# Row sums of squares as two fp32r products between the pair of tiles and the third tile

## The reference

```python
def rms_norm(x, g):
    xf = x.astype(jnp.float32)
    y = xf * lax.rsqrt(jnp.mean(xf * xf, axis=-1, keepdims=True) + EPS)
    return (y * g.astype(jnp.float32)).astype(x.dtype)

def sqrelu_mlp(h, w1, w2):
    return jnp.square(jax.nn.relu(h @ w1)) @ w2

def swiglu_ffn(x, w_in, w_out):
    gate, up = jnp.split(x @ w_in, 2, axis=-1)
    return (jax.nn.silu(gate) * up) @ w_out
# x = x + mixer(norm(x)); x = x + mlp(norm(x)); ... h = h + 0.5 * swiglu_ffn(rmsnorm(h, g), w_in, w_out)
```

## Time and profile before

| what | us |
|---|---|
| median of three runs | 1545.5 (1544.36 to 1545.63) |
| the profiled execution | 1544.45 |
| its span, from first to last instruction | 1542.7 |
| PE busy | 1530.5 |
| DVE busy | 1045.6 |
| ACT busy | 849.7 |
| DMA, busy share of 16 engines | about 56% |

### The profile page before, as it was taken

How to read it: one execution, slowest core, us unless ns; L and a number is a source line. 1 busy time by engine, 2 the same in 40 slices (tenths; PEclk the granted TensorE clock), 3 DMA queues, 4 the chain that set the end, 5 groups by cost and what they waited for, 6 DMA issues and landing times.

```text
span 1542.7 us, 34843 instructions
## 1 busy us (share of the span) xinstructions
PE 1530.5 (99%) x12794; PEld 1492.5 (97%) x12794; DVE 1045.6 (68%) x1766; ACT 849.7 (55%) x1302; POOL 122.5 (8%) x123
## 2 busy tenths in 40 slices
PE   9999999999999999999999999999999999999999
PEld 8899999988999999999999999999999998999999
DVE  7777765644876557666787766668576657787764
ACT  6776654546655445555445555556555547665543
POOL 1830000045000000000000000000000033200000
DMA  7156666554666665656665655656555972065564
GB/s 257 59 135 195 193 190 203 167 174 138 194 195 197 193 192 191 193 194 200 190 207 193 200 191 191 206 186 206 194 192 192 235 206 66 16 204 193 193 199 151
DMA packets 80783, 280.51 MB, mean 182 GB/s; under 512 B 8880, under 2 KB 12464, under 8 KB 80688
## 3 DMA queue, kind: packets, MB, share of 16 engines
q1 hardware_dynamic: 76512, 273.77, 55.8%
q10 hardware_dynamic: 4176, 5.38, 1.8%
HBM read 277.53 MB, written 1.57 MB: 181 GB/s over the span
## 4 chain that ended last, share of the span: by engine, by line
PE 94%; DVE 4%; ACT 1%; issue 1%; DMA 0%; SPq 0%; ACTq 0%; DVEq 0%
PE psum L1800 27%; PE psum L1804 27%; PE psum L1801 27%; PE psum L1948 2%; PE psum L1950 2%; PE psum L1949 2%; PE psum L2190 1%; PE psum L2239 1%; DVE w_lo L1067 1%; PE psum L2135 0%; DVE scratch L1664 0%; PE psum L2013 0%; PE psum L2223 0%; PE psum L2003 0%; DMA raw<-tiles 0%
## 5 line engine op out<-in xcount | busy, mean ns | idle before, releaser
L579 ACT ACTIVATE w_hi<-raw 128x1024 fp32r<-128x1024 f32 x515 | 544.1, 1059 | 474.8 <-PE psum L1804 437.2
L1067 DVE TENSOR_TENSOR w_lo<-raw,w_hi 128x1024 fp32r<-128x1024 f32 x480 | 587.2, 1224 | 251.8 <-ACT w_hi L579 251.5
L1800 PE MATMUL psum<-xs,w_hi 128*128 128x256 f32 x1904 | 528.8, 278 | 1.0 <-DVE w_lo L1729 0.8
L1801 PE MATMUL psum<-xs,w_hi 128*128 128x256 f32 x1904 | 526.0, 276 | 0.0
L1804 PE MATMUL psum<-xs,w_lo 128*128 128x256 f32 x1904 | 525.9, 276 | 0.0
L1800 PEld LDWEIGHTS psum<-xs,w_hi 128*128 128x128 f32 x1904 | 357.4, 188 | 2.1 <-DVE w_lo L1729 1.2
L1801 PEld LDWEIGHTS psum<-xs,w_hi 128*128 128x128 f32 x1904 | 357.4, 188 | 0.2
L1804 PEld LDWEIGHTS psum<-xs,w_lo 128*128 128x128 f32 x1904 | 357.3, 188 | 0.0
L1804 PE MATMUL psum<-hs,w_lo 128*128 128x256 f32 x1280 | 353.3, 276 | 0.0
L1800 PE MATMUL psum<-hs,w_hi 128*128 128x256 f32 x1280 | 353.3, 276 | 0.0
L1801 PE MATMUL psum<-hs,w_hi 128*128 128x256 f32 x1280 | 353.3, 276 | 0.0
(11 more groups left out here) (294 smaller groups left out, 1485.5 us busy)
## 6 DMA issues: line engine op xcount, KB each, us to landing
raw<-tiles SPq DMA_DIRECT2D x516, 512.0 KB, 4.2
bias<-bias_dram ACTq DMA_DIRECT2D x8, 256.0 KB, 6.1
w1c_all<-w1c_k ACTq DMA_DIRECT2D x4, 256.0 KB, 4.4
w1c_all<-w1c_v ACTq DMA_DIRECT2D x4, 256.0 KB, 6.1
y_out<-x SPq DMA_DIRECT2D x8, 128.0 KB, 3.4
con<-consts SPq DMA_DIRECT2D x1, 803.0 KB, 8.9
x<-x_in ACTq DMA_DIRECT2D x2, 256.0 KB, 4.8
raw<-tiles SPq DMA_DIRECT2D x2, 256.0 KB, 5.3
```

What stands on the lines that cost most here:

```text
L579: act.activation(slot_part(w_hi[s], t + RING * q if isinstance(q, int) else t), raw[s][:, :], ACT.Copy).then_inc(hi_ready, 1)
L1067: dve.tensor_tensor(slot_part(w_lo[s], t_), raw[s][:, :], hi_of(slot_part(w_hi[s], t_)), ALU.subtract).then_inc(lo_ready, 1)
L1800: pe.matmul(out, w_hi[s][:, c:c + P], x_hi, start=first, stop=False)
L1801: pe.matmul(out, w_hi[s][:, c:c + P], x_lo, start=False, stop=False)
```

## The change

Row sums of eight norms (not mix_0) become two fp32r products. ACT copies `ssq` as fp32r into `ssq_parts`, DVE subtracts it from `ssq` to get the rest, and PE multiplies a matrix of ones in fp32r with both, adding up in PSUM. `ssq_parts` uses the place of `scratch`, 64 bytes in, and `ones_r` is put so that it lies where weight buffers lie modulo 256 bytes. `sums` moves from ahead of the last six matmuls of `two()` to behind `two()`. The odd matmul is left out where a norm has no column sums. Column sums stay as they are.

```diff
+        with nc.sbuf_tensor("ssq_parts", [P, 16 + 2 * S], F32R) as ssq_parts:
+            ssq_parts = ssq_parts[:, 16:]
         scratch = sb("scratch", [P, 12 * S])
...
         ones = sb("ones", [P, P])
+        sb("apart_r", [P, 16])
+        ones_r = sb("ones_r", [P, P], F32R)
...
-        sb("apart", [P, 120])
+        sb("apart", [P, 104])
...
             def root(name):
+                if name in TO_ROWS and name != "mix_0":
+                    act.wait_ge(ssq_ready, SSQ0[name] + KD + 1)
+                    act.activation(ssq_parts[:, 0:S], ssq[:, :], ACT.Copy).then_inc(ssq_split, 1)
                 act.wait_ge(stat_done, STAT0[name])
...
             def norm(name):
+                if name in TO_ROWS and name != "mix_0":
+                    hi, lo = ssq_parts[:, 0:S], ssq_parts[:, S:]
+                    dve.wait_ge(ssq_split, 2 * TO_ROWS.index(name) - 1)
+                    dve.tensor_tensor(lo, ssq[:, :], hi_of(hi), ALU.subtract).then_inc(ssq_split, 1)
                 dve.wait_ge(std_ready, STD0[name])
...
+            dve.wait_ge(const_ready, 1)
+            dve.tensor_copy(ones_r[:, :], ones[:, :])
             dve.wait_ge(vec_loaded, 16)
...
                     if name in TO_ROWS:
-                        ins = pe.matmul(bank(RB, 0, S), ones[:, :], ssq[:, :], start=True, stop=True)
+                        if name == "mix_0":
+                            ins = pe.matmul(bank(RB, 0, S), ones[:, :], ssq[:, :], start=True, stop=True)
+                        else:
+                            pe.wait_ge(ssq_split, 2 * TO_ROWS.index(name))
+                            pe.matmul(bank(RB, 0, S), ones_r[:, :], ssq_parts[:, 0:S], start=True, stop=False)
+                            ins = pe.matmul(bank(RB, 0, S), ones_r[:, :], ssq_parts[:, S:], start=False, stop=True)
...
                     for k in range(KD):
                         pe.wait_ge(xs_ready, XS0[xs_name] + k + 1)
-                        if norm_ and k == KD - 1:
-                            sums(norm_)
                         for u in range(2):
...
                 if paired:
                     two()
-                if odd:
-                    odd_matmul()
+                    sums(norm_)
+                    if odd and norm_ in TO_COLUMNS:
+                        odd_matmul()
                 for u in range(2 if paired else 0, head):
```

More of the change, by code:

```diff
@@ L234, in build @@
         const_ready = sem("const_ready")
-        ssq_ready = sem("ssq_ready")
+        ssq_ready, ssq_split = sem("ssq_ready"), sem("ssq_split")
         stat_done, std_ready = sem("stat_done"), sem("std_ready")
```

## The result

The changed kernel takes 1551.85 us (median of 5, 1551.75 to 1553.04); the kernel before, beside it on the same chip, 1544.43 (1544.15 to 1545.63). The ratio is 1.0048, interval [1.0037, 1.0059]: **slower, by 7.4 us**, as in rival 1. Some runs of these kernels show a mean granted clock of 0.998 or 0.999 instead of 1.000 and take 1 to 3 us longer than the others of their set, so medians within a microsecond of each other are not told apart here, and lowest times are given where that matters.

The account below looks back on a forecast made before the run. PE's queue was taken as the bound, busy for 1530.5 of 1542.7 us. The terms -2.75 - 0.20 + 0.22 + 0.05 gave -2.7 us, so 1545.5 became 1542.8 us, range 1541.6 to 1553.5.

Parts of the forecast that it names:

- rival 1: From mid_0 to kvn, a wait at mid_0 leaves PE in the slow pace: 10.5 us more, 1553.3 us; chance 0.20.
- part 4: At mid_0, the split on ACT and DVE ahead of the products may delay the load of ones: 0.05 us lost.
- Part 1: In six row-sum stages, PE's queue loses the fp32 product and odd matmul: 0.46 us gained each, 2.75 us in six.
- Part 2: In kvn, two fp32r products hold PE 0.23 us instead of the fp32 product's 0.43: gain 0.20 us.
- Part 3: At mix_1, a 0.24 us gain becomes a 0.22 us loss, as PE waits about 0.45 us at the fifth tile.
- Part 5: In paired stages, the square root comes 0.47 us later, but fifth tiles apart from mix_1's have room: cost nothing.
- rivals 3 and 4: First: mix_1 regains the fast pace, 1542.1 us, chance 0.18; second: pair holds PE as long as fp32 product, 1544.4, 0.07.
- Rival 2: In every stage the product pair itself loses the fast pace: 8,300 matmuls, 37 us more, 1580 us; chance 0.05.
- Part 6: Copy of ones at the start: nothing, at most 0.4 us; tiles from eps to vc moved 64 bytes: nothing either way.

## Why the prediction was wrong

**The step that failed is part 4's cost: it put 0.05 us of lateness at mid_0 down as a loss of 0.05 us, and the runs show 10.25 us behind it.** The mechanism, its place and its price stood in the text, as rival 1 with a chance of 0.20. The lateness itself was right: the load comes 0.06 us late. From the last square to the load, ACT's lag, its copy, DVE's lag, its subtraction and the load's lag took 0.04, 0.42, 0.03, 0.42 and 0.12 us, where the prediction had 0.04 to 0.13, 0.42, 0.02, 0.42 and 0.05. But a margin of +0.01 to -0.08 says that the load is more likely late than not, and the reason given against rival 1, that it is a bubble of one step and no full stop, is no reason: 0.06 and 0.3 us of standing both ended slow at mid_0. The changed kernel's five times are all those of the slow pace. Of the two waits in dq one ended slow and one fast, so by the rows to hand rival 1 was about as likely as the forecast. That the wait would end slow at mid_0 could not be told from them.

- *Rival 1's price*: 2,370 matmuls and 10.5 us expected, 2,303 and 10.25 measured. Right.
- *Part 1*: the new products step by 113 ns, as taken. In the two runs without the late load the sum is seen by itself: medians 2.35 us under before (1542.31 against 1544.66), the lowest times 2.9 us (1541.38 against 1544.26), where the three parts without the 0.05 add up to -2.73. Right within what the times tell.
- *Part 2*: 0.24 us for kvn's pair, 0.23 expected. *Part 3*: 0.44 us of waiting at the fifth tile, 0.45 expected, and mqk stays slow; with the gain ahead of it, mix_1 costs 0.20 us, 0.22 expected. *Part 5*: no other fifth tile waits; the steps behind the pairs are even to the end of each stage. All right, and rivals 3 and 4 are out.
- *Rival 2* is what happens with either operand 64 bytes off, at the price given (1580 us expected, 1579.8 to 1580.7 measured). It did not happen because both operands lie in place; the reason given against it is what the runs confirm. Of rivals 1 and 2, which the prediction would let fall together if placement were of no interest, only this one hangs on placement; rival 1 came with every operand of the new products in place. The Trainium skill, "SBUF — State Buffer", section "Who interferes with whom", speaks of other engines on PE's ports and is not touched: here PE's own two operands decide. Both paces, 113.3 and 117.8 ns, lie above the estimate of 256 / 2.4 + 2.5 = 109.2 ns that the Trainium skill, "TensorE: Matmul & The Clock Gate", section "Back-to-back issue gap", gives for a single matmul; that section says itself that loads between matmuls change the figure.
- *Part 6* was right in its result and wrong in its reason. Moving ssq by 64 bytes costs the kernel before 37 us; it costs the changed kernel nothing. The likely reason, which no run tests, is that there no fp32 product of 256 columns reads ssq behind the fast pace any more.

What is still open: what in PE keeps one pace or the other, why the same wait at pre_0 and in dq ended in both, and whether an fp32 product ends the fast pace with its operands in place. The runs show when the pace changes, not by what.

## What to carry to other kernels

Where a kernel has two paces for one instruction, price a late operand by the pace it may leave behind, not by its own length: 0.06 us cost 10 us, and moving one addition ahead of another operation on DVE gave it back. If the margin of a moved step lies around zero, take the late case as the forecast and make room before the change is tried. And keep the place modulo 256 bytes of every operand that goes through a tuned stream of matmuls, also of those that only stand between: 64 bytes cost 37 us in four runs. Only shifts of 64 bytes were compared, so whether a shorter period than 256 would do is not shown.

## What was not expected of the hardware

- The pace outlives everything of its own kind: 2,303 matmuls and all tile borders from 759.17 to 1030.77 us. It was still there where matmuls of 512 columns came.
- Two fp32r products out of place lose the pace without one step over 0.12 us; and an odd matmul that turns it back can stop doing so when another operand moves by 64 bytes (1544.5 and 1581.3 us), at distances that agree within 0.01 us.
- The same wait, in the same code, can end in either pace: dq's last in two traces (117.7 and 113.6 ns over 22 steps), and pre_0's in one kernel (1558.9 us and some 1552, the latter by the time alone).
- The same instructions can turn the pace both ways: mix_1's sums and odd matmul turn fast into slow in the kernel before, and slow into fast where the six other odd matmuls are left out.
